# Two leading columns less in the gate, the retention output, the up-projections and the short convolution's output, with a new order in the first and the last stage

## What is computed

```python
def dwconv_valid(ext, w):
    W = w.shape[0]
    T = ext.shape[1] - W + 1
    acc = ext[:, 0:T] * w[0]
    for j in range(1, W):
        acc = acc + ext[:, j:j + T] * w[j]
    return acc

def shortconv_mixer(h, conv_state, w_in, conv_w, w_out):
    bg, cg, xin = jnp.split(h @ w_in, 3, axis=-1)
    u = cg * xin
    ext = jnp.concatenate([conv_state.astype(u.dtype), u], axis=1)
    y = dwconv_valid(ext, conv_w)
    return (bg * y) @ w_out, ext[:, -(CONV_WIDTH - 1):]

def conv_ffn(h, ffn_state, w_in, conv_w, conv_b, w_down):
    up, gate = jnp.split(h @ w_in, 2, axis=-1)
    ext = jnp.concatenate([ffn_state.astype(up.dtype), up], axis=1)
    a = dwconv_valid(ext, conv_w) + conv_b
    return (jax.nn.silu(a) * gate) @ w_down, ext[:, -(FFN_CONV_WIDTH - 1):]
...
    y_prompt = yp[:, N_META:]
```

## Time and profile before

| | us |
|---|---|
| median of 3 runs | 1484.68 |
| lowest, highest | 1484.41, 1485.56 |
| profiled execution | 1484.48 |
| its span, first to last instruction | 1482.7 |
| PE busy in it | 1474.0 (99%) |
| DVE busy, ACT busy | 773.7, 513.9 |
| mean granted clock of TensorE | 0.999 |

### The profile page before, as it was taken

One profiled execution on the slowest core, in us unless ns is written; L12 is line 12 of the kernel. 1 busy time (PEld: TensorE's weight loads), 2 busy tenths in 40 slices (PEclk: granted clock), 3 DMA queues, 4 the chain that ended last, 5 costly groups with the idle time before them and its releaser, 6 DMA issues.

```text
span 1482.7 us, 27481 instructions
## 1 busy us (share of the span) xinstructions
PE 1474.0 (99%) x11536; PEld 1403.2 (95%) x11536; DVE 773.7 (52%) x1039; ACT 513.9 (35%) x721; POOL 2.7 (0%) x21
## 2 busy tenths in 40 slices
PE   8999999999999999999999999999999999999998
PEld 8689869969987999999999999999999999999998
DVE  6666348437535965555552325445565555554232
ACT  5252154135215543333332313222343333333222
POOL 0000000000000000000000000000000000000000
PEclk9999999999999999999999999999999999999999
DMA  6543353263444332222222222223223222222321
GB/s 239 214 170 124 146 209 113 108 228 142 150 159 169 120 100 85 98 86 85 98 88 92 94 86 92 94 86 99 89 86 100 85 89 95 85 99 89 100 86 58
DMA packets 47456, 171.91 MB, mean 116 GB/s; under 512 B 5449, under 2 KB 5833, under 8 KB 46337
## 3 DMA queue, kind: packets, MB, share of 16 engines
q1 hardware_dynamic: 46912, 170.06, 33.0%
q10 hardware_dynamic: 432, 0.65, 0.1%
q0 software_dynamic: 32, 0.03, 0.0%
HBM read 149.39 MB, written 21.55 MB: 115 GB/s over the span
## 4 chain that ended last, share of the span: by engine, by line
issue 100%; POOL 0%; POOLq 0%
POOLq L106 0%; POOL ident L255 0%; POOL h_tail L252 0%; POOL ident L246 0%; POOL mean_v L248 0%; POOL dec_q_spread L263 0%; POOL h_lo L251 0%; POOL h_hi L250 0%; POOL mean_d L247 0%; POOL late_q_decayed L264 0%; POOL seed L257 0%; POOL seed L260 0%; POOL eps L249 0%; POOL seed L259 0%; POOL seed L258 0%
## 5 line engine op out<-in xcount | busy, mean ns | idle before, releaser
L837 ACT ACTIVATE w_hi<-w_raw 128x1024 fp32r<-128x1024 f32 x227 | 239.6, 1059 | 757.9 <-PE ps L389 476.6
L389 PE MATMUL ps<-h_hi,w_hi 128*128 128x264 f32 (+2 forms) x2304 | 469.8, 285 | 2.7 <-DVE h_lo L1126 2.7
L1101 DVE TENSOR_TENSOR w_lo<-w_raw,w_hi 128x1024 fp32r<-128x1024 f32 x227 | 276.6, 1221 | 369.8 <-ACT w_hi L837 369.6
L389 PE MATMUL ps<-h_lo,w_hi 128*128 128x264 f32 (+2 forms) x2304 | 466.9, 284 | 0.0
L389 PE MATMUL ps<-h_hi,w_lo 128*128 128x264 f32 (+2 forms) x2304 | 466.4, 284 | 0.0
L389 PEld LDWEIGHTS ps<-h_hi,w_hi 128*128 128x128 f32 x2304 | 357.2, 189 | 3.5 <-issue 2.8
L389 PEld LDWEIGHTS ps<-h_hi,w_lo 128*128 128x128 f32 x2304 | 356.7, 189 | 0.0
L389 PEld LDWEIGHTS ps<-h_lo,w_hi 128*128 128x128 f32 x2304 | 356.4, 189 | 0.0
L690 PE MATMUL ps<-z_hi,w_lo 128*128 128x264 f32 (+1 forms) x704 | 144.6, 283 | 0.0
L690 PE MATMUL ps<-z_lo,w_hi 128*128 128x264 f32 (+1 forms) x704 | 144.5, 283 | 0.0
L690 PE MATMUL ps<-z_hi,w_hi 128*128 128x264 f32 (+1 forms) x704 | 144.5, 283 | 0.0
(11 more groups left out here) (187 smaller groups left out, 1372.5 us busy)
## 6 DMA issues: line engine op xcount, KB each, us to landing
w_raw<-in_w_units_dram SPq DMA_DIRECT2D x227, 512.0 KB, 3.3
states<-in_state_ret_dram SPq DMA_DIRECT2D x32, 512.0 KB, 6.4
out_ret_s_dram<-states SPq DMA_DIRECT2D x32, 512.0 KB, 2.6
v_bcast<-v_scratch SPq DMA_DIRECT2D x8, 1024.0 KB, 5.8
out_ret_p_dram<-tmp SPq DMA_DIRECT2D x4, 512.0 KB, 4.4
out_y_prompt_dram<-y_rows SPq DMA_DIRECT2D x4, 512.0 KB, 2.6
x_res<-in_x_all_dram SPq DMA_DIRECT2D x6, 268.0 KB, 4.4
decay<-in_decay_dram SPq DMA_DIRECT2D x4, 287.0 KB, 4.9
```

Of the source, the lines that this page charges most:

```text
L389: out = mm(PS[:, 2 * s + half, at:at + n_col], a, b[:, lo:lo + n_col], start=first and n == 0, stop=last and n == 2)
L837: fn(WH[:, c % NS, :], RAW[:, c % NR, :], ACT.Copy).then_inc(hi_ready, 1)
L1101: tt(WL[:, c % NS, :], RAW[:, c % NR, :], WH[:, c % NS, :].bitcast(F32), ALU.subtract).then_inc(lo_ready, 1)
```

## The change

Two constants replace the old columns: `C_RET` is 10, and `C_FFN = (10, 14)` holds the first column of the up-projections. The gates of the feed-forward networks begin two columns behind them instead of four, which is the same column as before. In the short convolution the third product (the output gate) and the output projection start at column 14 instead of 12. Every other product keeps its width. `spans` now cuts 526 columns into 264 and 262, and 522 columns into 264 and 258.

The first stage loads the first quarter of unit 0 first, and a small tensor `mix_gain` (8 values for each partition) instead of `model_consts`; Q is computed for all eight x tiles alone, and K behind it as in the other heads. The last statistic is split in three: rows of both halves, and the eight running sequences apart in a bank of their own; the last row statistic adds its third and fourth square on PE instead of the third on DVE.

```diff
-C_RET = 8
+C_RET = 10
+C_FFN = (10, 14)
...
-FIN_STAT = (6, 1)
+FIN_STAT = (6, 1, 7)
...
-            sp.dma_start(RAW[:, 0, 0:512], w_all[0, :, 0:512]).then_inc(half_in, 16)
+            x_tile(0)
             x_tile(1)
             sp.dma_start(RAW[:, 0, 512:], w_all[0, :, 512:]).then_inc(raw_in[0], 16)
+            x_tile(2)
+            x_tile(3)
             in_heads(0, 1)
-            x_tile(3)
+            for k in range(4, KD):
+                x_tile(k)
             in_heads(0, 2)
-            x_tile(4)
-            in_heads(0, 3)
-            for k in range(5, KD):
-                x_tile(k)
             sp.dma_start(COS[:], io["cos"]).then_inc(tab_in, 16)
             sp.dma_start(SIN[:], io["sin"]).then_inc(tab_in, 16)
+            in_heads(0, 3)
+            sp.dma_start(CD[:], io["model_consts"]).then_inc(const_in, 16)
...
                 for k in range(KD):
-                    if k == 0:
-                        pe.wait_ge(half_lo, 1)
-                    elif k == 2:
-                        unit_ready(0)
-                    elif k == 4:
-                        unit_ready(2)
+                    if k < 2:
+                        pe.wait_ge(part_lo, k + 1)
+                    elif k % 4 in (0, 2):
+                        unit_ready(k // 4)
                     pe.wait_ge(h_lo, k + 1)
                     for e in range(2):
-                        out = part(2 * (k // 4), PAIR_A[e], k, e)
...
-                    if k >= K_LAG:
-                        n = k - K_LAG
-                        if n % 4 == 0:
-                            unit_ready(n // 2 + 1)
-                        part(2 * (n // 4) + 1, PAIR_B[0], n, 0)
...
+                pair_of_k(0, PAIR_B, 2, T // 2)
...
-                c0, n_in = (8, 528) if l == 0 else (12, 524)
-                w, wo = n_in // 2, (n_in - 4) // 2
+                c0, n_in = C_FFN[l], T - C_FFN[l]
+                w, wo = n_in // 2, (n_in - 2) // 2
...
-                    pair_of_k(c0 + 4, PAIR_B, u0 + 2, wo, 4, i)
+                    pair_of_k(c0 + 2, PAIR_B, u0 + 2, wo, 4, i)
...
                 y_rows(4, 1, range(4))
+                pe.wait_ge(fin_x, 7)
+                pe.wait_ge(fin_sum, 5)
+                row_squares(2, 1, first=True)
+                pe.wait_ge(fin_sq, 7)
+                row_squares(FIN_SQ[2], 1)
+                pe.wait_ge(fin_sq, 8)
+                row_squares(FIN_SQ[3], 1, last=True).then_inc(fin_stat, 1)
                 pe.wait_ge(fin_root, 1)
                 y_rows(6, 1, range(4, 8))
                 pe.wait_ge(rows_dve, 1)
                 y_rows(0, 2, range(4))
-                y_statistic(1)
                 pe.wait_ge(fin_x, 8)
+                sample_squares(2, first=True)
+                sample_squares(FIN_SQ[2])
+                sample_squares(FIN_SQ[3], last=True).then_inc(fin_stat, 1)
                 pe.wait_ge(fin_y, 8)
...
-                            pair_of_k(12, slots, U_SC_IN + n, w, 12, i)
+                            pair_of_k(14 if which == 2 else 12, slots, U_SC_IN + n, w - 1 if which == 2 else w, 12, i)
...
-                        out = three(slots[e], w, lhs_pair(c, kk, e), ZH[:, k, :], ZL[:, k, :], k == 0, k == KD - 1)
+                        out = three(slots[e], w - 1, lhs_pair(c, kk, e), ZH[:, k, 2:], ZL[:, k, 2:], k == 0, k == KD - 1)
...
-            act.dma_start(X[:, 0, :], io["x_all"][:, 0, :]).then_inc(x_in[0], 16)
-            act.dma_start(CD[:], io["model_consts"]).then_inc(const_in, 16)
-            act.dma_start(X[:, 2, :], io["x_all"][:, 2, :]).then_inc(x_in[2], 16)
+            act.dma_start(RAW[:, 0, 0:256], w_all[0, :, 0:256]).then_inc(part_in[0], 16)
+            act.dma_start(MIX[:], io["mix_gain"].rearrange("p k o -> p (k o)")).then_inc(mix_in, 16)
+            act.dma_start(RAW[:, 0, 256:512], w_all[0, :, 256:512]).then_inc(part_in[1], 16)
...
             fin_add(1, 3)
-            fin_sums(1, 2)
             dve.wait_ge(fin_t, 4)
             fin_rows(1, 0, 4)
             fin_rows(1, 1, 6)
+            dve.wait_ge(fin_root, 2)
+            dve.reciprocal(RN[:, 2:4], RN[:, 2:4]).then_inc(fin_rn, 1)
```

203 lines of the change are left out of this document (110 added, 93 removed).

## The result

The changed kernel takes 1491.16 us (median of 8 runs, 1489.41 to 1492.50); the kernel before, run beside it, 1484.52 us (8 runs, 1483.94 to 1485.56). The ratio is 1.0042, with an interval of 1.0033 to 1.0050: **slower by 6.6 us**, where 3.5 us less was forecast and where the range ended at 1483.4. The profiled execution takes 1491.23 us with a span of 1489.5, 6.8 more than the span in the earlier trace rows.

The account below looks back on a forecast made before the run. PE's matmuls were taken to bound nearly the whole kernel. Columns -1.8, start -1.2, clock -1.4 and end +0.9 sum to -3.5 us from 1484.68: 1481.2 us (chance 0.5), range 1480.0 to 1483.4.

Parts of the forecast that it names:

- Columns: Matmul loops on PE: two columns fewer in each of 2208 pairs, 4416 columns, would save 1.8 us.
- bounds of one sign: Limits for the saving from fewer columns: 1.2 us by the flat slope for all, 2.6 by the steep one.
- The width term: Matmul loops: narrower operands priced by slopes of 0.28 and 0.60 ns a column, 1.8 us less in all.
- Start: First stage: no wait for model_consts, so the first product comes at 6.6 us for 7.85, 1.2 us earlier.
- the 1.81 us of the prediction: First stage: time from the rounding of x tile 0 to PE's first product, expected to stay unchanged.
- Clock: First products on PE: 15 matmuls would run at 2.4 GHz instead of 1.2, 1.4 us less.
- the length of the idle stretch: PE ahead of its first product: idle 1.4 us instead of 2.66, taken as short enough to keep the clock.
- End: Last stage: six products ahead of block 1's second transposes delay it 1.2 us; the three stores end 0.9 us later.
- (a): First products: the clock falls all the same and the 15 slow matmuls stay; 1482.6 us, chance 0.33.
- (b): Last stage: stores don't wait for block 1, the earlier statistic gains up to 0.3 us; 1480.0 us, chance 0.12.
- (c): First stage: PE starves for unit 1 or late x tiles and the kernel gets slower; 1485.1 us, chance 0.05.
- DVE and ACT at nothing: Matmul loops: slightly smaller operands on these engines cost or gain nothing, since PE's work hides theirs.

Follow-up runs that it names:

- start-alone kernel: Kernel before at its old widths; operands of gate, up-projections' first units and short convolution's third product begin two columns later; 1491.60 us against 1484.67, ratio 1.0047.
- the sweep: Kernel before with operand starts (Q, K, gate) and part widths (retention output) varied by head, in two kernels; gate 2.8 and 2.3 ns a matmul more from columns 10 and 14.
- The run with the small load first: Kernel before with the changed first stage, 16 warm-up products for 10, and mix_gain issued ahead of the first weights; 1483.19 us against 1484.67, ratio 0.9987.
- first-stage kernel: Kernel before with only the changed first stage, load order and small mix_gain load; 1483.87 us against 1484.45, ratio 0.9994.
- last-statistic one: Kernel before with only the changed last statistic, row products ahead of the second transposes, samples' statistic behind; 1485.24 us against 1484.45, ratio 1.0006.

## Why the prediction was wrong

**Columns: wrong in sign, and this alone decides.** Forecast 1.8 us less, measured 6.1 more. The step that failed is "the starts at 8, 12 and 16 that the trace has don't differ by more than the slopes do, so I stay inside these ends". The three starts are all multiples of four, and 10 and 14 are not, so the rows could not speak of them. The prediction had said so of the widths ("parts of 262 and 258 columns, which are no multiples of four") and named the starts as unseen in the same sentence; it then set bounds of one sign, 1.2 to 2.6 us less. With an end above nothing the loss would have been a rival, and the sign of the sum would have hung on it: 3264 matmuls (by the short count of the start-alone kernel) make 3.3 us of each nanosecond.

The width term was off by itself: nothing or 0.8 us more in place of 1.8 less. The line through multiples of four was read rightly (the new rows at 520 and 512 columns fit its direction), but two columns are half a step. By the sweep 262 lies above that line, not on it: halfway between the 23.35 and 23.10 us of 264 and 260 would be 23.23, and the stretch takes 23.49, 2.8 ns a matmul of 262 more.

Between multiples of four fewer columns do cost less, though not evenly: 23.35 / 192 = 121.6 ns for 264 columns, 22.94 / 192 = 119.5 for 260, 22.78 / 192 = 118.6 for 256, so 3.0 ns for eight. The Trainium skill, page "TensorE: Matmul & The Clock Gate", section "Back-to-back issue gap", gives the gap of an isolated matmul as the columns at 2.4 GHz plus a constant of 2.5 ns, 3.3 ns for eight. In that difference the two outer rows nearly agree; in its size they don't, since an estimate by it for 264 columns is 112.5 ns. Also by it (an estimate), a part that loses two columns would gain 0.8 ns wherever it starts; the sweep shows otherwise for both, and it decides.

**Start: right in direction, mis-sized.** Forecast 1.2 us, measured 0.37. The step that failed is that x tile 0 would be late next and its rounding would start where ACT had started before, at 4.8 us. ACT starts there on the weights, which stand ahead of x in its order: they take it 0.42 us from 4.86. Then it waits 0.39 us for `mix_gain`, 4 KB landing 4.5 us behind their issue, hardly sooner than the 96 KB whose place they took (4.8 us). Together this is the 0.87 us from 4.8 to 5.67; from there on the 1.81 us of the prediction hold, and 5.67 + 1.81 is the 7.48 measured. I had read the size of the transfer, not its place in the queue. The run with the small load first shows that this wait can be taken away, and that nothing is gained while ACT rounds the weights first and they come later. Whether x rounded first would bring 6.6 us was not tried.

**Clock: a chance in a run, not a value.** Forecast 1.4 us as kept. In the profiled execution it fell, and the stage's 192 matmuls took 25.29 us, 1.5 more than the 23.77 with the clock kept. Of the 8 runs three lie at 1489.4 to 1489.7 and five at 1491.1 to 1492.5. The 1.6 us between the groups is the size of the term, and the profiled execution is one of the five; no profile was taken of one of the three, so that these kept the clock is argued, not shown. Their mean granted clock is noted as 1.000 and that of the five as 0.998 or 0.999, which fits; in the first-stage kernel the same note doesn't part the groups. The step that failed was to judge by the length of the idle stretch. It was 2.30 us here and not the 1.4 foreseen, since the first product came late; but the low clock also came behind 1.67 us of idling in the first-stage kernel, and not behind 1.81 in the last-statistic one. The rows at the kernel's end that the term leaned on were rows of the noted clock, which the first-stage kernel's stretch shows can say 1.00 at half pace. With 16 warm-up products and next to no idling, the first products ran at full pace in the profiles of all four kernels that have them, and the 11 runs of the first of these lie in one group. The Trainium skill, page "TensorE: Matmul & The Clock Gate", section "What's actually happening", has the number of slow matmuls vary from run to run of one kernel. The groups of times and the profiles with 0, some 14 and some 25 slow matmuls agree with that.

**End: right.** Forecast 0.9 us later, measured 0.8 in the changed kernel and 0.8 by the medians alone, by the way described: block 1 at 2.37 us for about 2.3, three stores back to back.

**Rivals.** (a) was what the profiled run did with the clock. (b) was wrong: the stores wait for block 1. (c) was wrong: PE waits for nothing in the first stage, and a slower outcome came from a side that none of the three named. DVE and ACT at nothing: right.

The sum with measured terms: +6.4 (loops) - 0.4 (start and first stage) + 0.8 (end) = +6.8, as in the spans.

## What to carry to other kernels

Where PE has no waits, the column at which a moving operand begins is part of the price of a matmul. For 4-byte operands of 256 to 268 columns, which is what was measured here, keep starts and widths at multiples of four columns, even at the cost of two idle columns, and price a new start or width from one stretch that has it, or leave both signs open. A small load behind a larger one on a busy queue can land as late as a larger load in its place (4 KB 4.5 us behind their issue, 96 KB 4.8); look at the landing time, not at the size, and at what stands ahead of its reader on the reader's own engine. And a gain that rests on the clock has to be secured by leaving PE nothing idle ahead of it, since the next run of the same kernel may not have it.

## What the runs showed that I had not expected

- Matmuls of 264 to 268 columns whose moving operand starts 4 bytes past a multiple of 16 cost 3.2 to 4.0 ns more than from such a multiple (counted from the tile's first column), 8 bytes past it 2.3 to 2.8, and 12 bytes past it nothing. No run shows why three is free where one and two aren't; that stays open. So does why start and width together cost less than the sum of each.
- A part of 262 columns is dearer than one of 264: 23.49 us for 23.35.
- The noted clock can be 1.00 over a stretch in which PE ran at half pace (14 matmuls in 3.05 us). The spacing of matmuls is the surer witness over a few microseconds.
- The old first stage doesn't gain from a kept clock, 25.27 us for 25.35, since PE then waits for its input. It does lose when the low clock lasts for 25 matmuls, 26.5 us.
